# Cache pages moved one by one by SyncE with their numbers in registers, in place of gathers by GpSimd

## What is computed

```python
full_kc = jnp.concatenate([ckp[page_table].reshape(DB, past, N_KV, HEAD_DIM), kc], axis=1)
full_vc = jnp.concatenate([cvp[page_table].reshape(DB, past, N_KV, HEAD_DIM), vc], axis=1)
ck, cend = _compress(full_kc, lp['cmp_pe_k'], lp['cmp_w1_k'], lp['cmp_w2_k'])
cv, _ = _compress(full_vc, lp['cmp_pe_v'], lp['cmp_w1_v'], lp['cmp_w2_v'])
...
kk = jnp.where(is_past, ksp[page, off, gi], ks[bi, pn, gi])
vv = jnp.where(is_past, vsp[page, off, gi], vs[bi, pn, gi])
```

## Time and profile before

| | |
|---|---|
| Median of 3 runs | 2198.21 us (2197.73 to 2203.45) |
| Profiled execution | 2206.82 us, its span 2205.1 us |
| Busy, share of the span | TensorE 73%, weight loads 33%, DVE 62%, ACT 14%, GpSimd 35% |
| Mean granted clock of TensorE | 0.774 |
| Stage attend | 227.5 to 417.6 us |
| Stage decode | 417.6 to 597.5 us |
| From 677 us to the end | route and experts |
| DMA, mean | 297 GB/s |

### The profile page before, as it was taken

How to read it: one execution, slowest core, us unless ns; L and a number is a source line. 1 busy time by engine, 2 the same in 40 slices (tenths; PEclk the granted TensorE clock), 3 DMA queues, 4 the chain that set the end, 5 groups by cost and what they waited for, 6 DMA issues and landing times.

```text
span 2205.1 us, 22198 instructions
## 1 busy us (share of the span) xinstructions
PE 1614.1 (73%) x7588; PEld 735.2 (33%) x7588; DVE 1369.7 (62%) x3392; ACT 305.4 (14%) x717; POOL 762.4 (35%) x915
## 2 busy tenths in 40 slices
PE   6998788668899468889767886566656766666665
PEld 5445664433667424545314442001000111101110
DVE  5999336412224657876456667965889544777555
ACT  3001235311102112221011010000000000000000
POOL 5910203551004732333233333343333333333332
PEclk9999878879999778899869887565566565656566
DMA  3111910252362199999999999999999999999997
GB/s 137 60 39 39 243 42 1 92 170 83 106 210 86 66 405 413 413 417 397 413 417 415 398 392 413 368 392 413 420 407 408 418 415 413 414 409 404 418 421 294
DMA packets 129900, 654.91 MB, mean 297 GB/s; under 512 B 22092, under 2 KB 37116, under 8 KB 59964
## 3 DMA queue, kind: packets, MB, share of 16 engines
q0 software_dynamic: 80000, 562.07, 63.3%
q1 hardware_dynamic: 49788, 91.42, 12.0%
HBM read 646.34 MB, written 11.26 MB: 298 GB/s over the span
## 4 chain that ended last, share of the span: by engine, by line
DMA 26%; PE 16%; DVE 12%; issue 7%; POOL 3%; ACT 0%; DVEq 0%; POOLq 0%; ACTq 0%
DMA ex_uv<-in_peer_uv,idxT 26%; PE ex_acc L2244 7%; DVE ex_uv L2366 5%; POOL ex_uv L2032 3%; PE ex_hb L2147 3%; PE ex_late L2217 1%; PE ex_late L2169 1%; DVE ch_ci L1689 1%; DVE ch_sc L1686 1%; PE ex_late L2197 1%; DVE ch_iu L1689 1%; PE ex_late L2184 1%; DVE ch_work L1723 1%; DVE ch_work L1726 1%; DVE ch_pick L1727 1%
## 5 line engine op out<-in xcount | busy, mean ns | idle before, releaser
L2366 DVE SCALAR_TENSOR_TENSOR ex_uv<-ex_uv,ex_hb 128x1024 f32<-128x1024 f32 x520 | 627.8, 1220 | 433.0 <-DMA ex_uv<-in_peer_uv,idxT 318.5
L2032 POOL DMA_INDIRECT ex_uv<-in_peer_uv,idxT x520 | 495.8, 954 | 920.4 <-PE ex_acc L2244 791.7
L2147 PE MATMUL ex_hb<-ex_h_rows,spread 24*128 24x512 bf16 x1040 | 346.5, 499 | 427.6 <-DVE ex_uv L2366 398.7
L2244 PE MATMUL ex_acc<-ex_uv,wts 128*32 128x512 f32 x2080 | 413.1, 937 | 0.8 <-DVE wts L2282 0.8
L2147 PEld LDWEIGHTS ex_hb<-ex_h_rows,spread 24*128 24x128 bf16 x1040 | 52.3, 99 | 757.3 <-DVE ex_uv L2366 601.1
L2485 ACT ACTIVATE ex_gelu<-ex_dots 128x4 f32<-128x4 f32 x130 | 26.8, 206 | 1122.9 <-DVE ex_uv L2366 1114.5
L2244 PEld LDWEIGHTS ex_acc<-ex_uv,wts 128*32 128x32 f32 x2080 | 71.7, 146 | 242.8 <-issue 240.2
L743 POOL TENSOR_TENSOR at_prob<-at_prob,at_coef 128x256 f32<-128x256 f32 (+3 forms) x32 | 40.1, 1254 | 103.9 <-DVE at_coef L853 103.9
L2217 PE MATMUL ex_late<-hx,ex_ring 128*128 128x264 f32 x256 | 69.1, 429 | 0.0
L1857 PE MATMUL ro_pq<-hT,w_q 128*128 128x256 f32 x256 | 60.1, 390 | 1.6 <-POOL idxT L1782 1.6
L2217 PEld LDWEIGHTS ex_late<-hx,ex_ring 128*128 128x128 f32 x256 | 52.7, 211 | 17.4 <-issue 7.2
(11 more groups left out here) (492 smaller groups left out, 2394.9 us busy)
## 6 DMA issues: line engine op xcount, KB each, us to landing
ex_ring<-in_late_w SPq DMA_DIRECT2D x24, 1024.0 KB
gate_ring<-in_w_in SPq DMA_DIRECT2D x6, 2048.0 KB, 9.1
ex_uv<-in_peer_uv,idxT POOLq DMA_INDIRECT x520
w_q<-in_peer_w_q SPq DMA_DIRECT2D x8, 1024.0 KB, 7.9
w_out<-in_w_out SPq DMA_DIRECT2D x2, 2048.0 KB, 17.2
ex_h_rows<-h_split SPq DMA_DIRECT2D x65, 48.0 KB
pr_x<-in_x_prompt SPq DMA_DIRECT2D x4, 512.0 KB, 5.0
gate_ring<-in_w_in_heads SPq DMA_DIRECT2D x1, 2048.0 KB
```

The source lines that it names most:

```text
L2032: pool.indirect_dma_start(uv[:, s % SLOTS].rearrange("p j n -> p (j n)"), None, table, bass.IndirectOffsetOnAxis(ap=S.idxT[:, t:t + 1], ax ...
L2147: last = pe.matmul(hb[s % 2][:, CHUNK * h:CHUNK * h + CHUNK], spread[p, k % LOAD, :], h_rows[p, l % 2, CHUNK * h:CHUNK * h + CHUNK], start ...
L2244: last = pe.matmul(acc[LANE * g:LANE * g + LANE, CHUNK * h:CHUNK * h + CHUNK], wts[:, s % (2 * BATCH), LANE - 1 - r:2 * LANE - 1 - r], uv[ ...
L2366: dve.scalar_tensor_tensor(out=rows_, in0=rows_, scalar=1.0, in1=hb[s % 2][:], op0=ALU.mult, op1=ALU.mult, accum_out=dots[:, B % 2, c:c + ...
```

## The change

GpSimd no longer fetches pages in these two stages. SyncE does, with one transfer of 64 KB for each page. The page table is loaded into one partition, and for each sequence SyncE loads its eight page numbers into registers (page_numbers) and issues eight transfers with the source address made from a register (load_pages). `pages` in 128 partitions, `part` and `row_of` with their instructions fall away.

In stage_attend the loads of L = 0 to 5 stand in SyncE's stream ahead of the stores of the new keys and values. In stage_decode they stand behind the first three windows. The loads of cache_v_sel are no longer a block after L = 13: sequence by sequence they follow the loads of cache_v_cmp (L = 8 to 15), which have the same numbers. The windows of values come ahead of L = 22, and the windows of keys of sequences 3 to 7 behind all pages. The buffers, the semaphore for each buffer and TensorE's order stay.

```diff
-def load_pages(pool, S, src, to, done, b):
-
-    for f in range(NPG // PACK):
-        pool.indirect_dma_start(to[:, PACK * f:PACK * f + PACK, :].rearrange("p i n -> p (i n)"), None, src,
-                                bass.IndirectOffsetOnAxis(ap=S.row_of[:, NPG // PACK * b + f:NPG // PACK * b + f + 1], axis=0))\
-            .then_inc(done, 16)
+def page_numbers(nc, io, S, b):
+
+    _, numbers = nc.values_load_multi_w_load_instructions(
+        S.pages[0:1, NPG * b:NPG * b + NPG], engines=[mybir.EngineType.SP], min_val=0, max_val=io["cache_v_sel"].shape[1] - 1,
+        skip_runtime_bounds_check_because="the page table holds numbers of the caches' pages")
+    return numbers
+
+
+def load_pages(sp, src, to, numbers, done):
+
+    n = P // PACK
+    for c, page in enumerate(numbers):
+        f, j = divmod(c, PACK)
+        sp.dma_start(to[n * j:n * j + n, PACK * f:PACK * f + PACK, :].rearrange("p i n -> p (i n)"),
+                     src[bass.ds(page * n, n), :]).then_inc(done, 16)
...
-            for b in range(NATS):
-                load_pages(pool, S, page_rows(io["cache_k_cmp"]), S.nat[:, b], S.nat_pool[b], b)
...
+            sp.wait_ge(E["pages_in"], 16)
+            for b in range(NATS):
+                load_pages(sp, page_rows(io["cache_k_cmp"]), S.nat[:, b], page_numbers(nc, io, S, b), S.nat_in[b])
...
-            dve.wait_ge(E["pages_in"], 16)
-            dve.wait_ge(E["parts"], PACK)
-            for j in range(PACK):
-                p = slice(P // PACK * j, P // PACK * j + P // PACK)
-                dve.scalar_tensor_tensor(out=S.row_of[p], in0=pages[p, j:NB * NPG:PACK], scalar=float(PAGE // PACK),
-                                         in1=part[p], op0=ALU.mult, op1=ALU.add).then_inc(E["rows_known"], 1)
...
-            for L in range(NATS, 3 * NB):
-                pool.wait_ge(E["tr_done"], turned[L - NATS])
-                cache = io[("cache_k_cmp", "cache_v_cmp", "cache_k_sel")[L // NB]]
-                load_pages(pool, S, page_rows(cache), nat[:, L % NATS], S.nat_pool[L % NATS], L % NB)
-                if L == NB + NATS - 1:
-                    for b in range(NB):
-                        load_pages(pool, S, page_rows(io["cache_v_sel"]), vsel[:, b], vlanded, b)
...
-            sp.wait_ge(E["hid_done"], 2)
-            for b in range(NB):
-                sp.dma_start(vwin[:, b].rearrange("p w n -> p (w n)"), v_win[:, b]).then_inc(E["wlanded"], 16)
+            for L in range(NATS, 3 * NB):
+                if L == 2 * NB + NATS:
+                    sp.wait_ge(E["hid_done"], 2)
+                    for b in range(NB):
+                        sp.dma_start(vwin[:, b].rearrange("p w n -> p (w n)"), v_win[:, b]).then_inc(E["wlanded"], 16)
+                numbers = page_numbers(nc, io, S, L % NB)
+                sp.wait_ge(E["tr_done"], turned[L - NATS])
+                cache = io[("cache_k_cmp", "cache_v_cmp", "cache_k_sel")[L // NB]]
+                load_pages(sp, page_rows(cache), nat[:, L % NATS], numbers, S.nat_in[L % NATS])
+                if NB <= L < 2 * NB:
+                    load_pages(sp, page_rows(io["cache_v_sel"]), vsel[:, L % NB], numbers, vlanded)
             for b in range(WINS, NB):
                 sp.wait_ge(E["tr_done"], turned[2 * NB + b - WINS])
                 sp.dma_start(kwin[:, b % WINS].rearrange("p w n -> p (w n)"), k_win[:, b]).then_inc(kwin_landed[b % WINS], 16)
```

More of the change, by code:

```diff
@@ L676, in stage_attend @@
         causal = sb("causal", [P, P])
-        pages = sb("pages", [P, NB * NPG], I32)
-        part = sb("part", [P, NB * NPG // PACK])
         cneg = sb("cneg", [P, NQ, NC_P])
@@ L699, in stage_attend @@
                  "ct_kept0", "ct_kept1", "s_done", "max_ready", "p_ready", "coef_ready", "scaled", "t_done", "pt0", "pt1",
-                 "pv_done", "o_kept", "stored", "gates_ready", "small_kept", "ck_zero", "pages_in", "parts", "rows_known",
+                 "pv_done", "o_kept", "stored", "gates_ready", "small_kept", "ck_zero", "pages_in",
                  "g_done", "g_kept")
@@ L730, in _ @@
             pool.wait_ge(E["masks"], 6)
-            for j in range(PACK):
-                if j:
-                    pool.wait_ge(E["parts"], j)
-                pool.iota(part[P // PACK * j:P // PACK * j + P // PACK, :], [[0, NB * NPG // PACK]], base=0, channel_multiplier=1,
-                          allow_small_or_imprecise_dtypes=True).then_inc(E["parts"], 1)
-            pool.wait_ge(E["rows_known"], PACK)
-            for b in range(NATS):
-                load_pages(pool, S, page_rows(io["cache_k_cmp"]), S.nat[:, b], S.nat_pool[b], b)
             for u, (i, r, j) in enumerate(UNITS):
@@ L749, in _ @@
             sp.dma_start(sin, io["rope_sin"]).then_inc(E["rope_in"], 16)
-            sp.dma_start(pages[:], io["page_table"].rearrange("b n -> (b n)").partition_broadcast(P)).then_inc(E["pages_in"], 16)
+            sp.dma_start(S.pages[:], io["page_table"].rearrange("(a b) n -> a (b n)", a=1)).then_inc(E["pages_in"], 16)
             for j, src in enumerate(("cmp_w1_k", "cmp_w1_v")):
@@ L1153, in stage_decode @@
         kwin_landed = [sem(f"kwin_landed{i}") for i in range(WINS)]
-        vlanded = S.gather_sem
+        vlanded = sem("de_vlanded")
         batches = [(a, b, f) for a in range(3) for b in range(NB) for f in range(0, NPG + (WT if a == 2 else 0), 4)]
@@ L1159, in arrivals @@
         def arrivals(L):
-            return 16 * (NPG // PACK) * (L // NATS + 1)
+            return 16 * NPG * (L // NATS + 1)
         block = open_block(nc, ctx, sems)
@@ L1368, in turn @@
                 if f == 0:
-                    pe.wait_ge(S.nat_pool[L % NATS], arrivals(L))
+                    pe.wait_ge(S.nat_in[L % NATS], arrivals(L))
                 if f == NPG:
@@ L1472, in _ @@
             pe.wait_ge(E["anT_kept"], 1)
-            pe.wait_ge(vlanded, 16 * NB * NPG // PACK)
+            pe.wait_ge(vlanded, 16 * NB * NPG)
             pe.wait_ge(E["wlanded"], 16 * NB)
@@ L2511, in build @@
         S.h_split = nc.dram_tensor("h_split", [TOK, 3, D], BF16).ap()
-        S.gather_sem = ctx.enter_context(nc.semaphore("gather_sem"))
-        S.nat_pool = [ctx.enter_context(nc.semaphore(f"nat_pool{i}")) for i in range(NATS)]
+        S.nat_in = [ctx.enter_context(nc.semaphore(f"nat_in{i}")) for i in range(NATS)]
         S.merge_w, S.out_w, S.route_w = ([ctx.enter_context(nc.semaphore(f"{n}_w{j}")) for j in range(k)]
@@ L2538, in build @@
                     S.nat = right(c2, "nat", [P, NATS, NPG, KVW])
-                    S.row_of = c2.enter_context(nc.sbuf_tensor("row_of", [P, NB * NPG // PACK], U32, side="right"))
+                    S.pages = c2.enter_context(nc.sbuf_tensor("pages", [1, NB * NPG], I32, side="right"))
                     S.gates = kb(c3, "gates", [P, TILES, 3 * NH])
```

## The result

The changed kernel took 2212.13 us (median of five runs, 2210.45 to 2215.49) against 2198.21 for the kernel before (five runs, 2197.64 to 2203.45): ratio 1.0058, with an interval of 1.0043 to 1.0073. It is slower, as predicted, but by 13.9 us (0.6%) and not by 43. Timed again beside the kernel before on two later chips, the ratio was 1.0043 (1.0027 to 1.0059) on one and 1.0171 (1.0150 to 1.0193) on the other. That the chips differ here turned out to be part of the answer. The profiled execution took 2210.45 us, with a span of 2208.7.

What follows compares the result with a forecast made beforehand. The unedited experts' stage (1,528 us) takes most time; in decode, SyncE's issue would make TensorE late. Prompt 0 plus decode 42.7 gives 43 us: 2249.5 against the profiled execution, 2241 against the median; range 2201 to 2295.

Steps and rivals of the forecast that it cites:

- d and r: SyncE's queue: its cost for one page transfer, taken as 0.60 us, and for one load of eight page numbers.
- rival 1: SyncE keeps pace and nothing changes: d at most 0.42 with r of 0.6, 2198 to 2204 us; chance 0.10.
- the lower edge of the forecast: Decode stage at d = 0.48 and r = 0.6: 13 us slower, 2211 us; the forecast to 2264 had chance 0.65.
- the formula: Decode stage: lateness is the larger of 10r + 136d - 58.3 and 18r + 208d - 101.9; 42.7 us.
- the first limit: Decode stage, L = 15: its pages land late for TensorE's turn 30, 10r + 136d - 58.3; 34.3 us late.
- The second: Decode stage, third pass: sequence 3's key window queues behind all pages, 18r + 208d - 101.9; 42.7 us late.
- Turn 30: TensorE's first turn of L = 15, second turning pass of decode; forecast near 520, 34.3 us late, behind a DMA.
- the window of sequence 3: Third decode pass: keys TensorE turned at 535.40, forecast there at 578.1, 42.7 us late, with TensorE waiting near 575.
- 58.3 and 101.9: Decode stage: constants in us subtracted from SyncE's queue time in the two lateness terms, 10r + 136d and 18r + 208d.
- Prompt stage: zero: Prompt attention: pages have some 150 us to arrive and the removed work is worth nothing at the end; 0 us.
- Rival 2: Turning passes: faster, as late copies may go without GpSimd's bursts; 9 us gained, 2189 us, below d of 0.40; chance 0.05.
- Rival 3: Register transfers much dearer: d = 0.9 and r = 1.6 give 114 us, 2312 us; chance 0.20 for all above 0.75.

Runs made afterwards that it cites:

- the queue by need: The changed kernel with SyncE's decode transfers in the order TensorE needs them, in two versions: 2187.74 us (0.9921) and 2183.61 us (0.9918).
- the moved block: Kernel before, block of 16 value gathers behind L = 21 instead of L = 13: 2200.13 us, 1.0009; with SyncE moving prompt-stage pages too: 2190.54 us, 0.9952.

## Why the prediction was wrong in size

*What bounds the kernel, experts' stage.* Right: 1607.1 us from the merge stage on in both (1603.7 to 1609.6 over all profiles), so what a stage wins or loses reaches the end.

*d and r.* The terms that were mis-sized. I took d = 0.60 and r = 1.1; the chip needs 0.487 for a page of keys, 0.452 for a page of values whose addresses are known, and 0.73 for a load. The nearest row that I chose, the 0.597 of a small transfer into 64 partitions, was the wrong neighbour: the issue itself is 0.316 to 0.370, near the plain ones of 0.328 and 0.364, and the register's arithmetic adds 0.046 and a move of 0.029, with gaps. No run shows a load of 1.1, and no row of the kernel before gave this value or the 0.6 of rival 1 and of the lower edge of the forecast. What the rows gave were landings of 2.8 and 1.5 us, again the wrong neighbours: a load takes 0.52 us (median of 24), 0.73 with its gaps.

*Decode stage.* The mechanism and the formula hold. With the measured costs the first limit is 10 x 0.73 + 80 x 0.487 + 56 x 0.452 - 58.3 = 13.3 us; the stage grew by 13.1. The second is 18 x 0.73 + 144 x 0.487 + 64 x 0.452 - 101.9 = 10.3 us by the formula, but 13.2 in the trace, where TensorE waits 1.06 us for that window: single issues of up to 1.22 us and loads of up to 0.74, which the sum leaves out, lengthened the queue. So the limits are within about a microsecond of each other, where I had the second 8 us above the first. Turn 30 came behind a DMA, but at 492 and not at 520; the window of sequence 3 at 539 and not at 575, in a stage that began 9.5 us earlier than in the kernel before. That both limits exist was shown by moving the values (the first gone, the second larger) and by the queue by need (0.9921 and 0.9918; on the second of these chips the changed kernel has 1.0043).

*The constants of the formula.* The 58.3 and 101.9 are TensorE's own times in the kernel before, and these held late copies. I read those and took them for a fixed part of the pass. They are a cost of the gathers: where they are absent the stage takes 158.9 us and not 180.3, so the late copies were some 21 us of it. The change trades them for the queue: 35.5 us of queue, of which 21.4 us of late copies are given back. The two figures come from different chips, and that the 21 us are late copies is read from the rows of both, not from a run that removes them alone. Without late copies turn 30 stood 50.7 us into the stage and not 69.8, so the constant of the first limit is 39.2 and not 58.3, and the formula gives 32.4 us at the measured costs, against 33.7 measured at turn 30. So on that chip the 38 us are near the 43 predicted by compensation, which is luck: my d and r were too large, and so was the constant that I took off.

*Prompt stage: zero.* The step that failed in kind. It asked only whether the pages and the removed work could be late, and they could not. It did not ask what the gathers did to others while they were issued. The late copies that I had read in the decode stage also stood beside the same gathers in this one. The stage became 8.9 us shorter on the first chip, 7.2 by an earlier start of the product and the rest by the granted clock in it (0.50 and 0.84 before, 1.00 after), and 1 us longer (181.1 to 182.0) on the chip without late copies.

*The sum.* It was 42.7 + 0. In the two profiles it was 13.1 - 8.9 us, and 13.9 as timed, since the profiled execution of before was 8.6 above its median and that of the changed kernel 1.7 below. The mis-sized d and r make 29 of the difference (42.7 less 13.3), and the prompt stage 9.

*The rivals.* Rival 1 needed d of 0.42: 0.487 is still too dear. Rival 2 had the right mechanism, late copies that go with the gathers. I gave it a price only where TensorE would be free to profit; in the prompt stage nothing else held it back, and in the decode stage it hid most of the queue's price. Rival 3 was far off. One page lands later than it is issued (1.8 us against 0.32), but 208 of them on one queue go at the pace of 0.45 to 0.49 us each, and this cost 35 us in one stage where no copy is late. Another 22 to 28 us lie between orders of the same queue (decode stages of 193.4, 171.6 and 165.9).

*What stays open.* How a run of gathers holds up an instruction of another engine that has its operand, and why on some chips and not on others: the rows call the releaser "remote" or name the finished product, and show no more. Profiles show it on four chips at least and its absence on one; a second chip without it is told by its time alone. Whether pacing prevents it while gathers are being issued was not seen either. Also open is why, on the first sort, the decode stage with gathers is 180.3, 183.2, 181.4, 179.0, 183.0 and 172.9 us in six profiles with a run of gathers in the prompt stage, and 174.3, 174.0, 176.8 and 175.3 in four without (172.9 and 175.3 with the moved block).

## What to carry to other kernels

When transfers move to one queue (SyncE's sent its 208 pages in the order of the program here), first write down the order in which the consumer needs them, and put what is needed last behind what is needed next: that was worth 22 to 28 us here, with the price of an issue as it was. When gathers go out back to back, read what the other engines do in that stretch, in every stage and also where the pages have time: a copy that starts microseconds after its operand is ready was a cost of the gathers here, and must not be counted as a fixed part of the pass. Before a difference of 1% is believed, time both kernels on more than one chip: the same change was 1.0043, 1.0058 and 1.0171 here, and the reordered one 0.9918 and 1.0037.

## What the runs showed of the hardware

- A transfer of 64 KB whose address is in a register costs SyncE 0.49 us (0.316 issue, 0.046 and 0.029 of register work, gaps), 0.45 where the address is computed already, and lands 1.7 to 4.1 us after its issue. A load of eight numbers from the on-chip memory takes 0.52 us (median), 0.73 with gaps.
- On four chips at least, while a run of indirect gathers went out on GpSimd, one each 1.25 us, hand-overs between TensorE, ScalarE and the DVE came late, by some 0.6 us to almost 10. They did with 256-byte rows too (DMA share 0.48 to 0.77), not with plain transfers at 365 to 392 GB/s, and not in the one stretch with two gathers under way and none being issued. On one chip the same run, at 399 GB/s, delayed nothing.
- Where TensorE stood idle between late copies (1.12 us busy of 4), its granted clock was 0.50, and the product behind took 9.64 us and not 7.81.
- The kernel before, with its gathers, took 2175 us on two chips and 2198 to 2206 on the others, while the changed kernel, which has no gathers in these stages, took 2210 to 2213 in all three timings.
